# First attention: turning a unit's probabilities one step later, and a two-scalar division for the sink heads

## The reference, cut to what matters

```python
# swa_attention (q in blocks of 128, keys of the block and the one before)
s = jnp.einsum('bnqgrd,bnkgd->bngrqk', qb, kb) * scale - slopes * dist      # masked to 0 <= dist < 128
m = jnp.maximum(jnp.max(s, axis=-1, keepdims=True), sg)                     # sg: the head's sink
e = jnp.exp(s - m)
prob = e / (jnp.sum(e, axis=-1, keepdims=True) + jnp.exp(sg - m))
o = jnp.einsum('bngrqk,bnkgd->bnqgrd', prob, vb)
# nsa_attention
o = gc[..., 0:1] * o_c + gc[..., 1:2] * o_s + gc[..., 2:3] * o_w            # each o_* is softmax(...) @ v
...
# behind both: x + rmsnorm(concat(nsa, swa) @ w_o), a gated MLP with a convolution, a second block
```

## Time and profile before

| | |
|---|---|
| three timed runs | 1309.13, 1309.33, 1311.11 us; median 1309.33 us |
| the profiled execution | 1308.19 us; its span, to which all rows belong, 1306.4 us |
| TensorE busy | 1272.6 us, 97% of the span |
| DVE, ACT, POOL busy | 785.3, 648.5 and 222.5 us |
| first attention (TensorE, first filling product of step 1 to the last values) | 69 to 250 us |
| TensorE's granted clock over the run | 0.994 of full speed |

### The profile page before, as it was taken

One profiled execution on the slowest core, in us unless ns is written; L12 is line 12 of the kernel. 1 busy time (PEld: TensorE's weight loads), 2 busy tenths in 40 slices (PEclk: granted clock), 3 DMA queues, 4 the chain that ended last, 5 costly groups with the idle time before them and its releaser, 6 DMA issues.

```text
span 1306.4 us, 16459 instructions
## 1 busy us (share of the span) xinstructions
PE 1272.6 (97%) x6004; PEld 1050.4 (80%) x6004; DVE 785.3 (60%) x1465; ACT 648.5 (50%) x1261; POOL 222.5 (17%) x234
## 2 busy tenths in 40 slices
PE   9997998999999999999999999999999999999998
PEld 8876787777888888888878877887888888888887
DVE  5677777486664556345778886589744343344335
ACT  6686767564344443233545655477543242242334
POOL 0065544300110011001002100022311020020111
PEclk9998999999999999999999999999999999999999
DMA  7211110143332333332322221342232323233331
GB/s 266 89 41 33 41 41 25 54 155 97 97 89 89 105 102 92 98 96 85 120 78 89 81 74 49 123 124 78 81 105 91 99 86 105 88 105 89 105 89 66
DMA packets 64625, 118.20 MB, mean 90 GB/s; under 512 B 7712, under 2 KB 12192, under 8 KB 64288
## 3 DMA queue, kind: packets, MB, share of 16 engines
q1 hardware_dynamic: 62704, 112.86, 28.4%
q10 hardware_dynamic: 1840, 4.29, 1.1%
HBM read 115.02 MB, written 2.10 MB: 90 GB/s over the span
## 4 chain that ended last, share of the span: by engine, by line
PE 88%; DVE 5%; POOL 3%; ACT 2%; issue 2%; DMA 1%; POOLq 0%; SPq 0%; DVEq 0%; ACTq 0%
PE bank L593 25%; PE bank L595 24%; PE bank L594 24%; PE bank L813 2%; POOL pp L2969 2%; PE bank L693 2%; PE bank L694 2%; PE bank L695 2%; PE bank L826 1%; PE bank L827 1%; POOL pp L2971 1%; PE bank L799 1%; PE bank L800 1%; PE bank L767 1%; DVE q2p L2191 0%
## 5 line engine op out<-in xcount | busy, mean ns | idle before, releaser
L2022 DVE TENSOR_TENSOR wl<-raw,wh 128x512 fp32r<-128x512 f32 (+2 forms) x360 | 267.9, 755 | 327.4 <-ACT wh L1323 326.7
L1323 ACT ACTIVATE wh<-raw 128x512 fp32r<-128x512 f32 (+1 forms) x398 | 242.2, 619 | 286.2 <-PE bank L595 273.9
L593 PE MATMUL bank<-AH,wh 128*128 128x512 f32 (+1 forms) x848 | 333.4, 393 | 2.1 <-DVE AL L2036 0.8
L595 PE MATMUL bank<-AH,wl 128*128 128x512 f32 (+1 forms) x848 | 328.9, 388 | 0.0
L594 PE MATMUL bank<-AL,wh 128*128 128x512 f32 (+1 forms) x848 | 326.5, 385 | 0.0
L593 PE MATMUL bank<-BH,wh 128*128 128x512 f32 x624 | 248.0, 397 | 0.0
L595 PE MATMUL bank<-BH,wl 128*128 128x512 f32 x624 | 244.9, 393 | 0.0
L594 PE MATMUL bank<-BL,wh 128*128 128x512 f32 x624 | 243.4, 390 | 0.0
L595 PEld LDWEIGHTS bank<-AH,wl 128*128 128x128 f32 x848 | 159.3, 188 | 35.7
L593 PEld LDWEIGHTS bank<-AH,wh 128*128 128x128 f32 x848 | 159.7, 188 | 35.0 <-issue 2.9
L594 PEld LDWEIGHTS bank<-AL,wh 128*128 128x128 f32 x848 | 159.5, 188 | 33.0 <-issue 0.2
(11 more groups left out here) (332 smaller groups left out, 1621.2 us busy)
## 6 DMA issues: line engine op xcount, KB each, us to landing
raw<-in_w_dn SPq DMA_DIRECT2D x104, 256.0 KB, 2.7
raw<-in_w_gu SPq DMA_DIRECT2D x88, 256.0 KB, 2.6
raw<-in_w_up SPq DMA_DIRECT2D x64, 256.0 KB, 2.6
raw<-in_w_nsa SPq DMA_DIRECT2D x16, 256.0 KB, 2.7
raw<-in_w_pg SPq DMA_DIRECT2D x16, 256.0 KB, 2.6
raw<-in_w_naq SPq DMA_DIRECT2D x16, 256.0 KB, 2.6
nbi<-in_na_bias ACTq DMA_DIRECT2D x8, 448.0 KB, 3.5
raw<-in_w_swa SPq DMA_DIRECT2D x10, 256.0 KB, 2.7
```

Source lines behind the costliest of these rows:

```text
L593: t.matmul(o, w, xh, start=start, stop=False, skip_group_check=skip)
L595: return t.matmul(o, wl, xh, start=False, stop=stop, skip_group_check=skip)
L1323: a.activation(W[i % NW].h[:, 0:n], RAW[i % NRAW][:, 0:n], ACT.Copy).then_inc(*s_wh.up(i))
L2022: v.tensor_tensor(w.l[:, 0:n], RAW[i % NRAW][:, 0:n], w.h[:, 0:n], ALU.subtract).then_inc(*s_wl.up(i))
```

## The change

Turn and values of a unit move one step later on all engines, and inside TensorE's step the turn now stands ahead of the scores. A step of TensorE is now: filling product, turn of unit s-2, scores of unit s+1, values of unit s-3. On VectorE `rest1` (of unit s-3) now stands ahead of `norm1` (of unit s-1). The loops of TensorE, ScalarE and VectorE get one more step, the product of `w_o_swa` 0 moves from step 12 to 13, since the output of the sink heads that it reads is complete one step later, and the division of the sink heads takes a second scalar, a column of ones.

```diff
-         10: [("w_nsa", 11)], 11: [("w_nsa", 12)], 12: [("w_o_swa", 0), ("w_nsa", 13)],
+         10: [("w_nsa", 11)], 11: [("w_nsa", 12)], 12: [("w_nsa", 13)], 13: [("w_o_swa", 0)],
...
-            for s in range(N_UNITS + 2):
+            for s in range(N_UNITS + 3):
                 if s < N_UNITS:
                     give_scores(s)
-                if s >= 2:
-                    give_turned(s - 2)
+                if s >= 3:
+                    give_turned(s - 3)
...
+                if 2 <= s <= N_UNITS + 1:
+                    turn1(s - 2)
                 if s + 1 < N_UNITS:
...
-                if 1 <= s <= N_UNITS:
-                    turn1(s - 1)
-                if s >= 2:
-                    values1(s - 2)
+                if s >= 3:
+                    values1(s - 3)
...
 # scalar: turned of s-2 (was s-1), out_part of s-3 (was s-2), out_high of s-4 (was s-3)
-                if 1 <= s <= N_UNITS:
-                    u = s - 1
+                if 2 <= s <= N_UNITS + 1:
+                    u = s - 2
...
 # vector: out_add of s-4 (was s-3), out_low of s-5 (was s-4)
+                if 3 <= s <= N_UNITS + 2:
+                    rest1(s - 3)
                 if 1 <= s <= N_UNITS:
                     norm1(s - 1)
...
-                if 2 <= s <= N_UNITS + 1:
-                    rest1(s - 2)
...
-                    if kind == "swa":
-                        m = g.tensor_scalar(o, o, r, None, ALU.mult)
-                    else:
-                        m = g.tensor_scalar(o, o, r, gate_of(u)[:, qb:qb + 1], ALU.mult, ALU.mult)
-                    m.then_inc(*s_nmg.up((u, qb)))
+                    by = ones[:, 0:1] if kind == "swa" else gate_of(u)[:, qb:qb + 1]
+                    g.tensor_scalar(o, o, r, by, ALU.mult, ALU.mult).then_inc(*s_nmg.up((u, qb)))
```

More of the change, by code:

```diff
@@ L1540, in scalar @@
             later = []
-            for s in range(N_UNITS + 3):
+            for s in range(N_UNITS + 4):
                 for name, i in later:
@@ L1579, in scalar @@
                         turned(SWA if kind == "swa" else NSA, u, PT[buf_of(u)], [s_pv.at(v)] if v >= 0 else [])
-                if s >= 2 and s - 2 < N_UNITS and closes(s - 2):
-                    key = out_key(s - 2)
+                if 3 <= s < N_UNITS + 3 and closes(s - 3):
+                    key = out_key(s - 3)
                     n = key[2] + (0 if key[1] == "swa" else 4)
-                    out_part(key, key[3], out_sum(key), s_pv.at(s - 2),
+                    out_part(key, key[3], out_sum(key), s_pv.at(s - 3),
                              *([s_xl.at(("ob", "swa", n - 2) if n < 6 else ("ob", "nsa", n - 6))] if n >= 2 else []))
-                if s >= 3 and closes(s - 3) and unit(s - 3)[2] == 1:
-                    pair = out_key(s - 3)[0:3]
+                if s >= 4 and closes(s - 4) and unit(s - 4)[2] == 1:
+                    pair = out_key(s - 4)[0:3]
                     out_high(pair, out_sum(pair), out_pair(pair), s_xl.at(("x0", 7)) if pair[1] == "swa" else s_cm.at(("hid", 1)))
@@ L2307, in vector @@
                     soft1(s)
-                if s >= 3 and closes(s - 3):
-                    key = out_key(s - 3)
+                if s >= 4 and closes(s - 4):
+                    key = out_key(s - 4)
                     out_add(key, key[3], out_sum(key))
-                if s >= 4 and closes(s - 4) and unit(s - 4)[2] == 1:
-                    pair = out_key(s - 4)[0:3]
+                if s >= 5 and closes(s - 5) and unit(s - 5)[2] == 1:
+                    pair = out_key(s - 5)[0:3]
                     out_low(pair, out_sum(pair), out_pair(pair))
+                if 3 <= s <= N_UNITS + 2:
+                    rest1(s - 3)
                 if 1 <= s <= N_UNITS:
```

## The result

The changed kernel takes 1287.78 us (median of four runs, 1285.56 to 1289.17), the kernel before 1309.68 (four runs, 1309.13 to 1311.11): ratio 0.983, 95% interval 0.981 to 0.985. It is 21.9 us faster. The profiled execution took 1286.42 us, its span is 1284.5 against 1306.4.

The account below looks back on a forecast made before the run. TensorE, 97% busy, bounds the kernel outside its gaps. Waits, restarts and clock gave a ceiling of 28.5 us, less 8.1 remaining: gain 20.4, profiled 1308.19 to 1287.8, median about 1289; range 1281 to 1299.

Parts of the forecast that it names:

- key wait: Step 9, a score waiting for the low part of the window keys: stays at about 2.8 us.
- Step 7: Turn of unit 5 waits for its last division tile, the small product for its bank: together 2.0 us.
- Step 14: Values of unit 11 wait for a w_o_swa product's bank, its copy standing behind unit 12's copies: 0.7 us.
- Steps 19 and 24: Turn right behind values waits for a w_o_swa product's bank; ScalarE copies head, then product: 1.2 us each.
- Steps 17, 20 and 25: Banks of scores written just before and remainders just in time: 0.2 us each, 0.6 in all.
- The last turn: Exponential, copies, remainders and division end 0.9 us behind the values of unit 25; before, 3.7 to 3.9 us.
- The load term: First attention stretch, TensorE, ScalarE and VectorE nearly full: 1.5 us added, bounds nothing and 10 us.
- Rival 4: Division length not due to its form, 1.4 us more per sink unit: 1291 us, chance 0.08.
- Rival 2: Bank and addition waits at steps 7, 14, 19, 24 are covered, clock stays up: 1283 us, chance 0.14.
- Rival 3: Late copies hold remainders and reciprocal, ScalarE's work sets steps 3 to 6: 1298 us, chance 0.18.
- Rival 5: Remainders ahead of the reciprocal close a loop over four engines: slower, 1317 us in its example, chance 0.06.
- The signs: In the changed profile: division waits under 4 us, bank waits 4 to 6, L2969 near 550 ns, VectorE/ScalarE above 85%.

Follow-up runs that it names:

- kernel 3: The changed kernel with the reciprocal (norm1) put back ahead of the remainders (rest1) in VectorE's step: 1287.83 us.
- kernel 4: The changed kernel with the turn, still of unit s-2, put back behind the scores in TensorE's step: 1293.37 us.
- Kernel 6: The changed kernel with ScalarE's copy of the w_o_swa product to acc moved earlier, into the product's own step: 1287.93 us.
- kernel 11: The changed kernel with the reciprocal ahead of the remainders and the acc copy in the product's own step: 1284.70 us.
- kernel 5: The changed kernel with the last filling product of the window keys moved from step 8 to step 7: 1289.39 us.

## Why the prediction was right, and where it was not

1289 was forecast and 1287.8 measured; the forecast gain of 20.4 us stands against 19.8 in the attention and 21.9 between the medians. The mechanism was the one named: the division's waits go, bank waits at ScalarE's and VectorE's copies come. But the agreement of the sum is closer than that of its terms. The same rule for both traces (each piece of TensorE from start to start, less what it takes where nothing waits) gives a loss of 34 to 35 us before and 14 to 15 after, depending on which starts are taken as undisturbed, where I had 31.3 and 10.9 with the key wait. So the residual was too small by 3 to 4 us and the ceiling by about as much. That they cancel is luck.

- **Step 7: forecast 2.0, measured 5.5.** The mis-sized term. The two waits are those named, 0.64 for the division and 0.39 for `os`. What is missing is the work of VectorE behind them, and a stretch at the lower level of the clock, 1.2 GHz, which I had priced for the ceiling and not for what remains:

```profile
100.07 0.33 PE L813 MATMUL bank<-ident,pp 128*128 128x128 f32 x1
101.04 1.51 PE L813 MATMUL bank<-ident,pp 128*128 128x128 f32 x6 [0.64 <-POOL pp L2969]
102.94 0.33 PE L790 MATMUL bank<-cw,chid 128*64 128x64 f32 x2 [0.39 <-DVE os L2214]
103.20 1.86 PE L843 MATMUL bank<-kc,qs 128*128 128x64 f32 x8
```

```profile
100.00:110.00 10.00, 8.77 (x36) 7.11 (x35) 9.02 (x23) 7.62 (x24) 6.58 (x10) 0.66 0.20 54
```

  Turn, compressed scores, values and filling product take 2.19, 0.82, 0.83 and 1.64 us more than undisturbed ones. 0.34 of 10 us, 3.4, is the clock. But little of this 3.4 is lost by the clock alone, for VectorE gives back the bank that the scores of step 8 need only at 111.36, and they start 0.37 us behind that:

```profile
110.48 0.88 DVE L2328 TENSOR_TENSOR vc<-bank,vc 31x64 fp32r<-31x64 f32 x4
111.73 0.48 PE L799 MATMUL bank<-ka_sl,qs 128*128 128x512 f32 x1
```

  VectorE itself waited 0.75 us for the slowed compressed scores. So at the upper level the scores of step 8 could have started some 1.1 us earlier at most (an estimate, 0.37 + 0.75). The rest of the 3.4 would have been a wait for `vc`, as in kernel 3. The walk had no row for that copy.
- **The key wait: forecast unchanged at 2.8, measured 1.6.** In kernel 4, with the turn behind the scores, it is 2.3: the turn of 0.7 us does cover, which I had ruled out. The other 0.5 us is not traced. The sum left this wait out on both sides, so 1.2 us of the gain were not forecast.
- **Step 14: forecast 0.7, measured 1.4,** not at the values of unit 11 but at the filling product that opens the step; what it waits for is the copy I named.
- **Steps 19 and 24: forecast 1.2 each, measured 1.31 and 1.30,** by the mechanism given: the head's copy, then the product's. Kernel 6 shows it.
- **Steps 17, 20 and 25: forecast 0.2 each.** Step 17 loses some 0.5 to 0.7 without a named wait, 20 and 25 nothing. In their place steps 22 and 27 lose 0.5 each to `acc` (0.3 us and a restart), which I had not seen.
- **The last turn: forecast 0.9, measured 1.0.**
- **The load term: forecast 1.5, spread over the sink heads.** No row needs it as a spread cost. What VectorE's full list costs stands in one place, ahead of the scores of step 8, and is part of the 5.5 us above.
- **Rival 4** (the division stays long) falls with it. **Rival 2** (nothing takes the waits' place) falls by the 4.9 us of waits for `acc` and `os`. **Rival 3** (ScalarE and VectorE the bound) does not hold for the changed kernel's time, but it holds in one place, at steps 7 and 8, and it is what stands behind the edits there that won nothing. Over 85 to 125 us VectorE is busy 37.3 of 40 us, before 31.1:

```profile
85.00:125.00 40.00, 37.20 (x214) 32.20 (x214) 37.31 (x103) 33.42 (x95) 21.48 (x28) 0.91 0.17 47
```

- **Rival 5** (the remainders ahead of the reciprocal make a loop that costs) falls as a reason for a slower kernel: with the reciprocal first the time is the same. But the order does cost once the acc copy is early: kernel 11 is 3.2 us faster than kernel 6 and its attention 2.5, where without that copy the attention gains 0.7.
- **The signs.** Those on the division, on `acc` and `os`, on the clock and on the part behind the attention came. The key wait (1.6, forecast 2 to 3.5), the mean of L2969 at 128x256 (649 ns, forecast near 550) and ScalarE's share of the sink stretch (84.5%, forecast above 85) did not.

What stays open: how far the full VectorE limits steps 5 to 9 as a whole. For kernel 3 its trace shows it up to the scores of step 8 (from 94 us on 97% busy, no wait listed). In the changed kernel VectorE still waits once in that stretch (0.75 us), and in kernel 5 for ScalarE (0.5 us). All edits there moved work or banks and none took work from VectorE, so what a lighter VectorE would win is not shown.

## What to carry to other kernels

Where a chain over four engines is late at TensorE in most steps, one more step between producer and user took the waits from 16.4 to 1.1 us, and it cut what a shorter producer wins from 5.3 to 2.3: price the two together. Behind it the next limit is who reads a PSUM bank last; put each copy where the engine would idle, not behind a copy that waits for unrelated work (alone this won nothing here, with the reciprocal first some 3 us), and write down after each reordering which piece draws which bank, since the order inside a step was worth 5.7 us, most of it by that. An edit that removes a wait where another engine is 93 to 97% busy may only rename the wait: measure the stretch, not the wait. The same holds for a stretch at the lower clock: it costs only what the next piece would not have waited for anyway (at step 7, 1.1 us at most of 3.4).

## What the runs showed of the hardware that was not expected

**A division that meets VectorE's subtractions is longer.** GpSimd in the changed kernel (four divisions to a row), then VectorE at the same times:

```profile
87.18 3.92 POOL L2969 TENSOR_SCALAR pp<-pp,small,ones 128x128 f32<-128x128 f32 x4 [0.34 <-DVE small L2272]
...
93.76 2.05 POOL L2969 TENSOR_SCALAR pp<-pp,small,ones 128x128 f32<-128x128 f32 x4 [1.40 <-DVE small L2272]
...
99.08 2.97 POOL L2969 TENSOR_SCALAR pp<-pp,small,ones 128x128 f32<-128x128 f32 x4 [2.00 <-DVE small L2272]
```

```profile
86.99 0.65 DVE L2104 TENSOR_TENSOR kb_sl<-tmp,ka_sl 64x512 fp32r<-64x512 f32 x1
...
96.31 1.32 DVE L2219 TENSOR_TENSOR BL<-os,BH 128x512 fp32r<-128x512 f32 x1
...
99.01 1.55 DVE L2109 TENSOR_TENSOR qs<-tmp,qs 64x512 fp32r<-64x512 f32 x2
```

The division takes 2.05 us where VectorE's work beside it reads PSUM, 2.97 beside two subtractions of queries, and 3.92 beside four of keys (86.99 to 89.77): some 0.46 us for each. The other way round, a subtraction of 0.67 us takes 1.32 when GpSimd's weight piece (95.78 to 97.08) has begun first. All of these subtractions read two operands outside PSUM. The Trainium skill (SBUF — State Buffer, SBUF: two separate sides) states an exclusive lock on a port pair that the two engines share, for VectorE's operations with two SBUF inputs. By that, the trace agrees in kind, for the instruction that begins second is the longer one; but the hold is 0.46 us beside a subtraction of 0.65 to 0.69 us, less than the whole of it. The step-7 division is the one of 2.97 us. Without its neighbours it would take 0.9 us less, more than the 0.64 us that it is waited for (an estimate; no run moved them).

**A stretch at the lower clock did not follow the same gap each time, and cost nothing where it came.** Kernels 3 and 11 have the same instructions up to step 12, and at step 7 the same single gap of 1.46 us ahead of the same product. The window 100 to 110 us of kernel 3 stands under its experiment, with a granted clock of 1.00. Of kernel 11 it is

```profile
100.00:110.00 10.00, 8.54 (x47) 7.24 (x46) 9.69 (x27) 8.11 (x25) 6.97 (x11) 0.83 0.20 55
```

So a stretch at the lower clock, worth 1.7 us of TensorE's time (0.17 of 10 us), comes or stays away in single executions of the same work. It cost nothing here. The scores of step 8, in kernel 3 at 110.27 us with a wait of 1.36 us for `vc`, start in kernel 11 at

```profile
110.52 0.50 PE L799 MATMUL bank<-ka_sl,qs 128*128 128x512 f32 x1
```

with no wait, and `vc` is ready at 110.47. From L767 both are 56.1 us. Here VectorE was the later engine, and the lower clock only filled TensorE's wait for it.
